# RG-LRU gates with high and low parts stacked in 128 rows, in a two-layer hybrid attention / RG-LRU / MLP step

## The chip, the cores and the metric

One core of one Trainium2 chip runs the whole step as one program. The metric is device time in microseconds (us); the kernel before takes 2474.3 us, the median of three runs (2474.01 to 2475.89).

## The reference

The step takes 1024 prompt frames, 32 frames of a running stream and 16 meta tokens through two layers. Each layer is: RMSNorm, one input projection, two parallel head groups, an output projection with a residual, then RMSNorm and a squared-ReLU MLP with a residual. One head group is latent attention. The other, the RG-LRU, is where the change lies:

```python
xc = p["conv_b"] + sum(xpad[:, k:k + T] * p["conv_w"][k] for k in range(CONV_W))
xb = xc.reshape(B, T, LRU_BLOCKS, LRU_BW)          # 8 blocks of 64 channels
r = sigmoid(einsum("btnc,ncd->btnd", xb, p["w_gate_a"]).reshape(B, T, LRU_W) + p["b_gate_a"])
i = sigmoid(einsum("btnc,ncd->btnd", xb, p["w_gate_x"]).reshape(B, T, LRU_W) + p["b_gate_x"])
log_a = -LRU_C * r * softplus(-p["lru_lambda"])
a = exp(log_a)
b = sqrt(-expm1(2.0 * log_a)) * (i * xc)
h_t = a_t * h_{t-1} + b_t                           # then y = h * gelu(g_r)
```

The two gates r and i are block-diagonal products: 8 blocks of 64 channels, each with its own 64 x 64 matrix for r and another for i.

## The kernel before

**Layout and precision.** All tokens of both request groups lie side by side as T = 1074 columns (1072 tokens and 2 columns of padding); channels lie on the 128 partitions. A product in fp32 is made of three fp32r passes (`PASSES`, L921): high weights by high data, high by low, low by high. "High" is the operand copied to fp32r, "low" what that copy left over. Each pass goes over the 1072 columns in three matmuls of 358, 358 and 356.

**Weight blocks.** Weights come in numbered blocks through two buffers, block b in buffer b % 2. SyncE loads a block to `raw_all` once the low half of the block before last is done, ScalarE copies its high half (`split`, L1496, semaphore `w_hi`) once TensorE is through with block b - 2, and VectorE subtracts for its low half (`split`, L2193, `w_lo`). `product` (L947) waits for the low half of its block, then for its place in PSUM, and makes all its passes.

**Units and slots.** The products of the mixer are numbered units. Units alternate between two PSUM slots of three banks each; `take(u)` (L931) makes unit u wait until unit u - 2 was read from the slot (the table `READ`). Banks 6 and 7 hold sums of squares.

**Order in the stretch of the gates** (the same in each layer; every engine has its own order written out by hand): TensorE runs the x_r products (XR), two gate-branch products (GR0, GR1), `gates(0)`, GR2, GR3, `gates(1)`, two latent products (CKV0, CKV1), `gates(2)`, the rotary-key product (`kr_product`, L1040: 48 matmuls on one block), CQ0, `gates(3)`, CQ1, CQ2, then a sum of squares for the latent (`sum_of_parts`, L988) and CQ3 to CQ5. A full product has 72 matmuls. c in `gates(c)` counts tiles of 128 channels, so each holds two blocks of 64: an even and an odd one.

**gates(c), L1006:** two products with a 128 x 128 weight each, one for r and one for i, with the two 64 x 64 matrices on the diagonal and zeros elsewhere: 2 x 3 x 3 = 18 matmuls, each gate in a slot of its own.

**ScalarE** (L1511 to L1618): `gate_r(c)` reads r from PSUM (Tanh, L1524), then makes Tanh (L1526) and Exp (L1528); `gate_i(c)` reads i (L1533) and makes a Sqrt (L1534, after a load of the activation table); `xc_hi(c+1)` makes the high part of the next tile of `xc`; `gelu_a`, `gelu_b` belong to the GeLU branch; `kr_lo` (L1606) reads half of the rotary keys; `split(b)` stand in between. **VectorE** (L2250 to L2391): `xc_lo(c)` (L2221) makes the low part of `xc`; `lru(c)` (L2258 to L2268) makes b and runs the scan; `scaled` evicts a product from PSUM (L2216); the eviction of the rotary keys (L2372, `kr_ev`) frees the slot that `gates(3)` takes next. **GpSimd** makes the GeLU's polynomial (`cube`, L3166 and L3168) for each tile.

**Between the layers** VectorE (L3105 to L3118) finishes the sums of squares of the new x with `next_sum(4..7)` (L3103) and then `next_split(1)` (L3096), the low half of layer 1's second weight block, for which TensorE's second product there waits.

Of the kernel before, what the change touches and what calls it, by code (L numbers as in the profile page):

```python
# [191 lines left out]

U_XR, U_GR, U_GATE, U_CKV = [0, 1, 2, 3], [4, 5, 8, 9], [6, 10, 14, 18], [12, 13]
U_KR, U_CQ = 16, [17, 20, 21, 22, 23, 24]
U_UQ, U_K, U_V = [25, 26, 27, 28, 29, 30], 31, 35
U_OY, U_OO, U_MLP = [45 + _c for _c in range(8)], 53, 61
NU = U_MLP
# [24 lines left out]
for _c in range(4):  # L222
    READ[U_XR[_c]] = ("xr_ev", _c + 1)
    READ[U_GR[_c]] = ("gr_ev", _c + 1)
    READ[U_GATE[_c]] = ("gate_r", _c + 1)
    READ[U_GATE[_c] + 1] = ("gate_i", _c + 1)
    READ[U_UQ[2 + _c]] = ("qn", _c + 1)
    READ[U_K + _c] = ("kf", _c + 1)
# [13 lines left out]
for _c in range(4):  # L242
    LAST_UNIT[B_XR[_c]] = U_XR[_c]
    LAST_UNIT[B_GR[_c]] = U_GR[_c]
    LAST_UNIT[B_GATE[_c]] = U_GATE[_c] + 1
    LAST_UNIT[B_OO + _c] = U_OO + 2 * _c + 1
# [171 lines left out]
def trunk(nc, xT, wst, vec, fgain, ropeC, ropeS, ident_in, past_ckv, past_kpe, h0, conv0,  # L418
          yT, ckv_out, kpe_out, h_out, conv_out, x_scr, sum_scr):
    ctx = ExitStack()  # L420
    with ctx:
# [17 lines left out]
        def tiles(name, region, first, n, dt=F32):  # L439
            return [place(f"{name}{i}", region, (first + i) * TB, T, dt) for i in range(n)]  # L440
# [479 lines left out]
        def _(pe):  # L920
# [5 lines left out]
            for L in range(DEPTH):  # L926
# [20 lines left out]
                def product(dst, u, b, woff, rhs_h, rhs_l, ready=None):  # L947

                    w("w_lo", b + 2)
                    take(u)  # L950
                    n = len(rhs_h)
                    for k in range(n):
                        if ready:
                            ready(k)
                        for i, (a, c) in enumerate(PASSES):
                            wt = (whi if a == "h" else wlo)[b % 2][:, woff + 128 * k:woff + 128 * k + 128]
                            r = (rhs_h if c == "h" else rhs_l)[k]
                            for q in range(3):
                                mm = nc.tensor.matmul(dst(q), wt, r(q), start=(k == 0 and i == 0), stop=(k == n - 1 and i == 2))  # L959
                    mm.then_inc(S["mm"], 1)  # L960
# [44 lines left out]

                def gates(c):  # L1006
                    w("xc_lo", c + 1)
                    for k in range(2):
                        product(to_slot(U_GATE[c] + k), U_GATE[c] + k, B_GATE[c], 128 * k, [tok(xch)], [tok(xcl)])

# [446 lines left out]
        def _(act):  # L1457
# [28 lines left out]
            for L in range(DEPTH):  # L1486
# [24 lines left out]
                def xc_hi(c):  # L1511
                    w("conv", c + 1)
                    if c:
                        w("mm", U_GATE[c - 1] + 2)
                    nc.scalar.activation(xch[:, :], xc[c][:, :], ACT.Copy).then_inc(S["xc_hi"], 1)

                def gate_r(c):

                    w("mm", U_GATE[c] + 1)
                    if c:  # L1520
                        w("hid", c)
                    else:
                        w("conv", 4)
                    nc.scalar.activation(chunks(t1), slot(U_GATE[c]), ACT.Tanh, scale=0.5, bias=half_ba[:, c:c + 1]).then_inc(S["gate_r"], 1)  # L1524
                    w("gate_r", c + 1)
                    nc.scalar.activation(t3[:, :], t1[:, :], ACT.Tanh, scale=sp2[:, c:c + 1], bias=sp2[:, c:c + 1]).then_inc(S["gate_y"], 1)  # L1526
                    w("gate_y", c + 1)
                    nc.scalar.activation(t1[:, :], t1[:, :], ACT.Exp, scale=neg_sp4[:, c:c + 1], bias=neg_sp4[:, c:c + 1]).then_inc(S["gate_t"], 1)  # L1528

                def gate_i(c):  # L1530

                    w("mm", U_GATE[c] + 2)
                    nc.scalar.activation(chunks(t4), slot(U_GATE[c] + 1), ACT.Tanh, scale=0.5, bias=half_bx[:, c:c + 1]).then_inc(S["gate_i"], 1)  # L1533
                    nc.scalar.activation(t3[:, :], t3[:, :], ACT.Sqrt).then_inc(S["root_t"], 1)  # L1534
# [49 lines left out]
                gate_r(0)  # L1584
                split(8)
                gate_i(0)
                xc_hi(1)
                split(9)
                gelu_a(0)
                gelu_b(0)  # L1590
                split(10)
                gate_r(1)
                split(11)
                gate_i(1)
                xc_hi(2)
                split(12)
                gelu_a(1)
# [5 lines left out]
                xc_hi(3)  # L1603
                split(15)
                w("mm", U_KR + 1)
                nc.scalar.activation(chunks(kpe[0:64, :]), slot(U_KR)[64:128], ACT.Copy).then_inc(S["kr_lo"], 1)  # L1606
                gelu_a(2)
                gelu_b(2)
                split(16)
                gate_r(3)  # L1610
                split(17)
                gate_i(3)
                for c in range(2):
# [527 lines left out]
        def _(dve):  # L2141
# [34 lines left out]
            for L in range(DEPTH):  # L2176
# [73 lines left out]
                def xc_lo(c):  # L2250
                    w("xc_hi", c + 1)
                    lo(xcl[:, :], xc[c][:, :], xch[:, :], "xc_lo")

# [94 lines left out]
                scaled(U_GR[1], g[1], rs, "gr_ev", LIVE)  # L2348
                split(7)
                split(8)  # L2350
                xc_lo(1)
                lru(0)
                split(9)
                scaled(U_GR[2], g[2], rs, "gr_ev", LIVE)
                scaled(U_GR[3], g[3], rs, "gr_ev", LIVE)
                split(10)
                gelu(0)
                split(11)
                xc_lo(2)
                lru(1)  # L2360
                split(12)
                scaled(U_CKV[0], ckv[0][:, 0:T], rs, "ckv_ev")
                scaled(U_CKV[1], ckv[1][:, 0:T], rs, "ckv_ev")
# [3 lines left out]
                xc_lo(3)  # L2367
                lru(2)
                split(15)
                w("mm", U_KR + 1)  # L2370
                w("kr_lo", 1)
                V.tensor_tensor(chunks(kpe[0:64, :]), slot(U_KR)[0:64], chunks(kpe[0:64, :]), ALU.add).then_inc(S["kr_ev"], 1)  # L2372
                scaled(U_CQ[0], cq[0], rs, "cq_ev", LIVE)
                split(16)
                gelu(2)
# [678 lines left out]
                def closing():  # L3054
# [30 lines left out]
                    if L < DEPTH - 1:  # L3085
# [386 lines left out]
```

## Time and profile before

| | |
|---|---|
| runs | 2474.01, 2474.3, 2475.89 us |
| the profiled execution | 2474.88 us, its span 2473.1 us |
| mean granted TensorE clock | 0.998 |

The span goes from the first to the last instruction; the execution's own time is 1.8 us more. In rows of the timeline the columns are start (us), length (us), engine, line, operation, output <- input, shapes, count, and in brackets the idle time before it with what ended it. Matmuls overlap: a matmul of 358 columns is listed with some 0.33 us, but the next starts much earlier, so their cost is read from one start to the next.

### The profile page before, as it was taken

To read this page: it belongs to the slowest core of one execution; us is meant where nothing else is said; L and a number is where in the kernel's file an instruction comes from. 1 tells how busy PE (TensorE), PEld (TensorE's weight loads), DVE (VectorE), ACT (ScalarE), POOL (GpSimd) and SP (SyncE) were. 2 spreads that over 40 slices of the span, in tenths; PEclk is the share of its full clock that TensorE was granted. 3 is DMA by queue.
4 is the path that set the end of the run, shared out by engine and by line. 5 is a ranking of instruction groups with operands and counts; after the bars stand their busy time and mean duration, and the time that the engine had idled before them with its cause. 6 is when DMAs were issued, how large, how long until landed. Compare 5 with 4: busy or idle time off the path is not lost.

```text
span 2473.1 us, 43928 instructions
## 1 busy us (share of the span) xinstructions
PE 2455.4 (99%) x17424; PEld 2371.3 (96%) x17424; DVE 1800.1 (73%) x2778; ACT 1219.7 (49%) x2197; POOL 515.9 (21%) x478
## 2 busy tenths in 40 slices
PE   9999999999999999999999999999999999999998
PEld 9999977899999999999999999779999999999997
DVE  8678767579776777677676797674887766776676
ACT  5455355535554454455524643555355544554455
POOL 0024255200112211220201232541001112211222
PEclk9999999999999999999999999999999999999999
DMA  4122201212447634663721222012135456545655
GB/s 160 55 60 73 61 11 38 86 59 107 89 91 140 122 86 99 135 119 89 226 89 52 63 70 61 11 38 90 60 115 103 91 120 131 110 89 115 131 113 173
DMA packets 104537, 230.39 MB, mean 93 GB/s; under 512 B 14816, under 2 KB 17984, under 8 KB 104336
## 3 DMA queue, kind: packets, MB, share of 16 engines
q0 software_dynamic: 43648, 89.14, 20.4%
q1 hardware_dynamic: 60544, 138.42, 17.6%
q8 instruction: 139, 2.28, 0.4%
q14 instruction: 62, 0.51, 0.1%
q10 hardware_dynamic: 144, 0.04, 0.0%
HBM read 144.03 MB, written 81.18 MB: 91 GB/s over the span
## 4 chain that ended last, share of the span: by engine, by line
PE 95%; DVE 3%; issue 1%; ACT 0%; DMA 0%; DVEq 0%; POOL 0%; ACTq 0%; POOLq 0%
PE ps L959 27%; PE ps L1303 23%; PE ps L1352 23%; PE ps L1167 5%; PE ps L1182 4%; PE ps L1444 3%; PE ps L1237 2%; PE ps L1415 2%; PE ps L1114 2%; PE ps L1026 1%; PE ps L1139 1%; DVE mxp L2518 0%; PE ps L1441 0%; PE ps L988 0%; DVE xall L2777 0%
## 5 line engine op out<-in xcount | busy, mean ns | idle before, releaser
L2808 DVE TENSOR_TENSOR wlo<-raw_all,whi 128x512 fp32r<-128x512 f32 (+1 forms) x420 | 270.9, 653 | 178.2 <-ACT whi L1973 175.7
L1973 ACT ACTIVATE whi<-raw_all 128x512 fp32r<-128x512 f32 (+1 forms) x420 | 248.6, 600 | 278.8 <-DVE raw_all L2941 87.8
L3307 POOL DMA_DIRECT2D x_scratch<-stage x224 | 199.6, 942 | 838.7 <-DVE stage L2951 694.3
L2026 ACT ACTIVATE stage<-ps 128x536 f32<-128x536 f32 (+1 forms) x224 | 135.4, 612 | 148.5 <-PE ps L1352 142.8
L1496 ACT ACTIVATE whi<-raw_all 128x1024 fp32r<-128x1024 f32 (+3 forms) x72 | 66.7, 926 | 233.9 <-PE ps L959 231.6
L2951 DVE TENSOR_TENSOR stage<-stage,ps 128x536 f32<-128x536 f32 (+1 forms) x168 | 119.0, 708 | 85.5 <-PE ps L1352 84.5
L2518 DVE TENSOR_REDUCE mxp<-ps 64x1 f32<-64x64 f32 (+11 forms) x384 | 140.4, 372 | 54.7 <-PE ps L1114 48.2
L959 PE MATMUL ps<-xgh,whi 128*128 128x358 f32 (+1 forms) x720 | 157.5, 327 | 1.8 <-DVE wlo L3096 1.7
L959 PE MATMUL ps<-xgl,whi 128*128 128x358 f32 (+1 forms) x720 | 156.6, 326 | 0.0
L959 PE MATMUL ps<-xgh,wlo 128*128 128x358 f32 (+1 forms) x720 | 156.5, 325 | 0.0
L959 PEld LDWEIGHTS ps<-xgh,whi 128*128 128x128 f32 x720 | 123.3, 189 | 2.6 <-DVE wlo L3096 2.0
L959 PEld LDWEIGHTS ps<-xgl,whi 128*128 128x128 f32 x720 | 124.1, 189 | 0.0
L959 PEld LDWEIGHTS ps<-xgh,wlo 128*128 128x128 f32 x720 | 123.3, 189 | 0.0
L2193 DVE TENSOR_TENSOR wlo<-raw_all,whi 128x1024 fp32r<-128x1024 f32 (+3 forms) x70 | 87.3, 1247 | 41.0 <-ACT whi L1496 40.6
L1167 PE MATMUL ps<-pn,v 128*65 128x320 f32 (+1 forms) x288 | 106.3, 453 | 0.0
L1754 ACT ACTIVATE pn<-ps 128x320 f32<-128x320 f32 (+1 forms) x144 | 65.4, 454 | 71.4 <-PE ps L1182 70.0
L1182 PE MATMUL ps<-qo,koh 128*128 128x320 f32 (+7 forms) x304 | 97.0, 400 | 0.0
L1182 PE MATMUL ps<-qe,keh 97*128 97x320 f32 (+7 forms) x304 | 95.7, 396 | 0.7 <-DMA qe<-mt 0.7
L2941 DVE TENSOR_TENSOR raw_all<-raw_all 128x256 f32<-128x256 f32 x224 | 89.7, 420 | 4.0 <-DMA raw_all<-in_wst 2.9
L1754 ACT ACTIVATE pd<-ps 16x64 f32<-16x64 f32 (+4 forms) x352 | 56.8, 224 | 55.4 <-PE ps L1182 55.1
L3292 POOL DMA_DIRECT2D raw_all<-in_wst x30 | 29.8, 992 | 254.2 <-DMA raw_all<-in_wst 254.2
L1182 PEld LDWEIGHTS ps<-qe,keh 97*128 97x128 f32 x304 | 54.7, 190 | 26.2 <-issue 7.2
(835 smaller groups left out, 7684.3 us busy)
## 6 DMA issues: line engine op xcount, KB each, us to landing
raw_all<-in_wst SPq DMA_DIRECT2D x232, 256.0 KB, 3.4
raw_all<-in_wst SPq DMA_DIRECT2D x80, 512.0 KB, 3.6
x_scratch<-stage POOLq DMA_DIRECT2D x112, 268.0 KB, 6.2
x_scratch<-stage POOLq DMA_DIRECT2D x112, 264.0 KB, 6.0
x_scratch<-xall POOLq DMA_DIRECT2D x24, 537.0 KB, 3.4
xall<-x_scratch SPq DMA_DIRECT2D x24, 537.0 KB, 9.4
xall<-in_xT SPq DMA_DIRECT2D x16, 537.0 KB, 7.2
raw_all<-in_wst POOLq DMA_DIRECT2D x30, 256.0 KB, 5.1
```

What stands on the lines that cost most here:

```text
L959: mm = nc.tensor.matmul(dst(q), wt, r(q), start=(k == 0 and i == 0), stop=(k == n - 1 and i == 2))
L1167: mm = nc.tensor.matmul(ps[0:65, bank, c0:c0 + n], v[:, v0:v0 + 65], p_tile(gk)[:, 0:n], start=(k in FIRST), stop=(k in LAST))
L1182: mm = nc.tensor.matmul(ps[:, gi % 3, 0:n], ks[e][0 if a == "h" else 1][rows, k0:k0 + P], qs[e][0 if c == "h" else 1][rows, q0:q0 + n], st ...
L1303: mm = nc.tensor.matmul(ps[:, 2 * slot_ + t, 0:HN], wt, rhs[:, t * HN:(t + 1) * HN], start=(opens and n == 0), stop=(n == 11), skip_group_ ...
L1352: mm = nc.tensor.matmul(ps[:, 2 * slot_ + t, 0:HN], ring(u, whi if a == "h" else wlo)[:, wc], fop[q, f + c][:, t * HN:(t + 1) * HN], start ...
L1754: ins = nc.scalar.activation(dst[r0:r1, c0:c1], src[r0:r1, c0:c1], ACT.Exp, scale=SM_SCALE)
L1973: nc.scalar.activation(dst, src, ACT.Copy).then_inc(S["u_hi"], 1)
L2026: nc.scalar.activation(quarters(stage_of(L, g, i, n)[:, 0:N2]), src, ACT.Copy, scale=-1.0 if row else 1.0).then_inc(S["x_copy"], 1)
L2518: ins = V.reduce_max(mxp[lo_:hi_, tile, part:part + 1], ps[lo_:hi_, max_bank(h, s), c0:c0 + n], AX_X)
L2808: V.tensor_tensor(dst, src, hi.bitcast(F32), ALU.subtract).then_inc(S["u_lo"], 1)
L2951: V.tensor_tensor(st, st, src, op).then_inc(S["x_add"], 1)
L3307: pool.dma_start(x_scr[2 * i + row, :, a:b], stage_of(L, g, i, n)[:, 0:b - a], accum_op=ALU.add).then_inc(S[done], 16)
```

## The change

The high and the low part of 64 channels of `xc` are stacked in 128 rows (`x_even` and `x_odd`, on the buffers of `xch` and `xcl`), against weights that hold the same 64 x 64 matrix twice, one above the other; the even block's weight has r and i side by side in its 128 columns, the odd block's has i and r. One pass with the high weights and one with the low ones then give both gates of 64 channels: 12 matmuls for `gates(c)` in place of 18. The odd block's results stand in the unit's slot; the even block's stand in banks 6 and 7 (512 columns each) and, for the last 48, in the rest of the slot's third bank. `gates(c)` is one unit, not two, so units are renumbered. Because r and i of a tile now lie half in one place and half in another, each gate is read by three ScalarE instructions (`gate`), `xc_hi` and `xc_lo` take two instructions each, and ScalarE reads both gates before it goes on with Tanh and Exp (`decay`) and Sqrt (`normal`). The orders of ScalarE and VectorE in the stretch are moved about. `product` waits for the high half of its block first and for the low half only before its third pass. Between the layers `next_split(1)` goes ahead of `next_sum(7)`. The diff, without the renumbering and the packing of weights and biases on the host:

```diff
@@ -626,6 +626,12 @@
 def half(e):
     return slice(64 * e, 64 * e + 64)
+
+
+def even_gates(c, end):
+
+    rest = ps[:, 3 * slot_of(U_GATE[c]) + 2, CH:CH + end - SUM_END]
+    return (ps[:, 6, :], 0, 512), (rest, SUM_END, end), (ps[:, 7, :], 512, SUM_END)
@@ -946,13 +952,15 @@
         def product(dst, u, b, woff, rhs_h, rhs_l, ready=None):
-            w("w_lo", b + 2)
+            w("w_hi", b + 1)
             take(u)
             n = len(rhs_h)
...
                     ready(k)
                 for i, (a, c) in enumerate(PASSES):
+                    if k == 0 and a == "l":
+                        w("w_lo", b + 2)
                     wt = (whi if a == "h" else wlo)[b % 2][:, woff + 128 * k:woff + 128 * k + 128]
                     r = (rhs_h if c == "h" else rhs_l)[k]
@@ -1004,9 +1012,21 @@
         def gates(c):
+            u, b = U_GATE[c], B_GATE[c]
             w("xc_lo", c + 1)
-            for k in range(2):
-                product(to_slot(U_GATE[c] + k), U_GATE[c] + k, B_GATE[c], 128 * k, [tok(xch)], [tok(xcl)])
+            w("w_lo", b + 2)
+            take(u)
+            if c:
+                w("gate_i", c)
+            else:
+                w("root", SUM_MIX)
+            for i, part in enumerate((whi, wlo)):
+                for dst, c0, c1 in even_gates(c, TOK):
+                    nc.tensor.matmul(dst, part[b % 2][:, 0:P], x_even[:, c0:c1], start=(i == 0), stop=(i == 1))
+            for i, part in enumerate((whi, wlo)):
+                for q in range(3):
+                    mm = nc.tensor.matmul(to_slot(u)(q), part[b % 2][:, P:2 * P], tok(x_odd)(q), start=(i == 0), stop=(i == 1))
+            mm.then_inc(S["mm"], 1)
         if L == 0:
@@ -1511,8 +1531,18 @@
             w("conv", c + 1)
             if c:
-                w("mm", U_GATE[c - 1] + 2)
-            nc.scalar.activation(xch[:, :], xc[c][:, :], ACT.Copy).then_inc(S["xc_hi"], 1)
+                w("mm", U_GATE[c - 1] + 1)
+            for e, dst in ((0, x_even), (1, x_odd)):
+                ins = nc.scalar.activation(dst[half(e), :], xc[c][half(e), :], ACT.Copy)
+            ins.then_inc(S["xc_hi"], 1)
+
+        def gate(c, dst, e, bias):
+
+            rest = even_gates(c, T)[1][0]
+            nc.scalar.activation(dst[0:64, 0:SUM_END].rearrange("p (c n) -> p c n", c=2), ps[half(e), 6:8, :], ACT.Tanh, scale=0.5,
+                                 bias=bias[half(e), c:c + 1])
+            nc.scalar.activation(dst[0:64, SUM_END:T], rest[half(e)], ACT.Tanh, scale=0.5, bias=bias[half(e), c:c + 1])
+            return nc.scalar.activation(chunks(dst[64:128, :]), slot(U_GATE[c])[half(1 - e)], ACT.Tanh, scale=0.5, bias=bias[half(1 - e), c:c + 1])
         def gate_r(c):
@@ -1521,16 +1551,21 @@
             else:
                 w("conv", 4)
-            nc.scalar.activation(chunks(t1), slot(U_GATE[c]), ACT.Tanh, scale=0.5, bias=half_ba[:, c:c + 1]).then_inc(S["gate_r"], 1)
+            gate(c, t1, 0, half_ba).then_inc(S["gate_r"], 1)
+
+        def gate_i(c):
+
+            gate(c, t4, 1, half_bx).then_inc(S["gate_i"], 1)
+
+        def decay(c):
+
             w("gate_r", c + 1)
             nc.scalar.activation(t3[:, :], t1[:, :], ACT.Tanh, scale=sp2[:, c:c + 1], bias=sp2[:, c:c + 1]).then_inc(S["gate_y"], 1)
...
             nc.scalar.activation(t1[:, :], t1[:, :], ACT.Exp, scale=neg_sp4[:, c:c + 1], bias=neg_sp4[:, c:c + 1]).then_inc(S["gate_t"], 1)
-        def gate_i(c):
-
-            w("mm", U_GATE[c] + 2)
-            nc.scalar.activation(chunks(t4), slot(U_GATE[c] + 1), ACT.Tanh, scale=0.5, bias=half_bx[:, c:c + 1]).then_inc(S["gate_i"], 1)
+        def normal(c):
+
             nc.scalar.activation(t3[:, :], t3[:, :], ACT.Sqrt).then_inc(S["root_t"], 1)
@@ -1582,17 +1617,21 @@
         split(7)
         gate_r(0)
-        split(8)
         gate_i(0)
         xc_hi(1)
+        split(8)
+        decay(0)
+        normal(0)
         split(9)
         gelu_a(0)
...
         split(10)
         gate_r(1)
-        split(11)
         gate_i(1)
         xc_hi(2)
+        split(11)
+        decay(1)
+        normal(1)
         split(12)
         gelu_a(1)
@@ -1601,15 +1640,19 @@
         gate_i(2)
         xc_hi(3)
-        split(15)
         w("mm", U_KR + 1)
         nc.scalar.activation(chunks(kpe[0:64, :]), slot(U_KR)[64:128], ACT.Copy).then_inc(S["kr_lo"], 1)
+        decay(2)
+        normal(2)
+        split(15)
         gelu_a(2)
         gelu_b(2)
         split(16)
         gate_r(3)
+        gate_i(3)
         split(17)
-        gate_i(3)
+        decay(3)
+        normal(3)
         for c in range(2):
             w("ckv_ev", c + 1)
@@ -2144,6 +2187,7 @@
     for s in (0, 1):
         V.memset(ps[:, 3 * s + 2, CH - 2:CH], 0.0)
+        V.memset(ps[:, 3 * s + 2, CH + TOK - 1024:CH + T - 1024], 0.0)
     V.memset(mx[:, :], 0.0).then_inc(S["const_set"], 1)
     lam = vecs[:, V_LAM:V_LAM + 4]
@@ -2249,7 +2293,8 @@
         def xc_lo(c):
             w("xc_hi", c + 1)
-            lo(xcl[:, :], xc[c][:, :], xch[:, :], "xc_lo")
+            V.tensor_tensor(x_even[half(1), :], xc[c][half(0), :], x_even[half(0), :].bitcast(F32), ALU.subtract)
+            V.tensor_tensor(x_odd[half(0), :], xc[c][half(1), :], x_odd[half(1), :].bitcast(F32), ALU.subtract).then_inc(S["xc_lo"], 1)
         def lru(c):
@@ -2347,31 +2392,31 @@
         scaled(U_GR[1], g[1], rs, "gr_ev", LIVE)
         split(7)
+        xc_lo(1)
         split(8)
-        xc_lo(1)
+        scaled(U_GR[2], g[2], rs, "gr_ev", LIVE)
         lru(0)
         split(9)
-        scaled(U_GR[2], g[2], rs, "gr_ev", LIVE)
         scaled(U_GR[3], g[3], rs, "gr_ev", LIVE)
         split(10)
         gelu(0)
+        xc_lo(2)
         split(11)
-        xc_lo(2)
+        scaled(U_CKV[0], ckv[0][:, 0:T], rs, "ckv_ev")
         lru(1)
         split(12)
-        scaled(U_CKV[0], ckv[0][:, 0:T], rs, "ckv_ev")
         scaled(U_CKV[1], ckv[1][:, 0:T], rs, "ckv_ev")
         split_kr()
...
         split(14)
         xc_lo(3)
-        lru(2)
-        split(15)
         w("mm", U_KR + 1)
         w("kr_lo", 1)
         V.tensor_tensor(chunks(kpe[0:64, :]), slot(U_KR)[0:64], chunks(kpe[0:64, :]), ALU.add).then_inc(S["kr_ev"], 1)
+        lru(2)
+        split(15)
+        split(16)
         scaled(U_CQ[0], cq[0], rs, "cq_ev", LIVE)
-        split(16)
         gelu(2)
         split(17)
@@ -3113,9 +3158,10 @@
                 next_sum(3)
                 next_low(7)
-                for m in (4, 5, 6, 7):
+                for m in (4, 5, 6):
                     next_sum(m)
                 next_split(1)
+                next_sum(7)
             else:
                 for n in range(6, 24):
```

## Rows read from the trace of the kernel before

**Rows 1.** The page's part 1: busy time, share of the span, instructions.
```profile
PE 2455.4 (99%) x17424; PEld 2371.3 (96%) x17424; DVE 1800.1 (73%) x2778; ACT 1219.7 (49%) x2197; POOL 515.9 (21%) x478
```

**Rows 2.** Timeline, TensorE, layer 0: gates(0) starts, GR2 starts.
```profile
80.30 1.14 PE L959 MATMUL ps<-xcs,whi 128*128 128x358 f32 x6
...
83.48 0.65 PE L959 MATMUL ps<-xgh,whi 128*128 128x358 f32 x3
```

**Rows 3.** Timeline, TensorE: starts of gates(2), kr, CQ0, gates(3), CQ1, sum.
```profile
133.86 1.14 PE L959 MATMUL ps<-xcs,whi 128*128 128x358 f32 x6
...
137.03 0.65 PE L1046 MATMUL ps<-xgh,whi 128*128 128x358 f32 x3
...
144.92 0.65 PE L959 MATMUL ps<-xgh,whi 128*128 128x358 f32 x3
...
156.97 1.23 PE L959 MATMUL ps<-xcs,whi 128*128 128x358 f32 x6
...
160.04 0.73 PE L959 MATMUL ps<-xgh,whi 128*128 128x358 f32 x3
...
183.73 1.23 PE L988 MATMUL ps<-xcs,ones_r 128*128 128x512 f32 x6
```

**Rows 4.** Timeline, TensorE, layer 1: gates(3) starts.
```profile
1388.03 1.22 PE L959 MATMUL ps<-xcs,whi 128*128 128x358 f32 x6 [0.15 <-DVE kpe L2372]
```

**Rows 5.** Timeline, TensorE, layer 0: fp32r matmuls of 512 and 50 columns, then XR2.
```profile
32.42 0.40 PE L988 MATMUL ps<-msq_r,ones_r 128*128 128x512 f32 x1
32.66 0.19 PE L988 MATMUL ps<-rs_r,ones_r 128*128 128x50 f32 x1
...
32.97 0.76 PE L959 MATMUL ps<-xgh,whi 128*128 128x358 f32 x3
```

**Rows 6.** Timeline, all engines, between the layers.
```profile
1244.13 5.42 DVE L3103 TENSOR_TENSOR msq<-msq,next_sq 128x1074 f32<-128x1074 f32 x4
...
1248.35 0.65 PE L959 MATMUL ps<-xgh,wlo 128*128 128x358 f32 x3
1249.47 1.22 DVE L3096 TENSOR_TENSOR wlo<-raw_all,whi 128x1024 fp32r<-128x1024 f32 x1
...
1250.74 0.76 PE L959 MATMUL ps<-xgh,whi 128*128 128x358 f32 x3 [1.75 <-DVE wlo L3096]
```

**Rows 7.** Groups by line and shape, ScalarE, 80 to 190 us: busy us, mean ns.
```profile
L1496 ACT ACTIVATE whi<-raw_all 128x1024 fp32r<-128x1024 f32 x10 | 10.5, 1052 | 26.4 <-PE ps L959 26.4
L1526 ACT ACTIVATE t<-t,sp 128x1074 f32<-128x1074 f32 x4 | 5.2, 1289 | 0.1
...
L1534 ACT ACT_TABLE_LOAD x4 | 5.1, 1283 | 0.1
...
L1524 ACT ACTIVATE t<-ps,half_ba 128x1074 f32<-128x1074 f32 x4 | 4.6, 1161 | 1.8 <-PE ps L959 1.8
...
L1534 ACT ACTIVATE t<-t 128x1074 f32<-128x1074 f32 x4 | 4.4, 1104 | 0.0
...
L1606 ACT ACTIVATE kpe<-ps 64x1074 f32<-64x1074 f32 x1 | 1.1, 1070 | 0.0
L1559 ACT ACTIVATE sqa<-ps,eps 128x50 f32<-128x50 f32 x1 | 0.3, 292 | 0.0
```

**Rows 8.** Timeline, VectorE, layer 0: lru(2), split(15), lru(3), the sum's low part.
```profile
145.96 1.27 DVE L2258 SCALAR_TENSOR_TENSOR t<-t,t 128x1074 f32<-128x1074 f32 x1
...
155.22 0.43 DVE L2193 TENSOR_TENSOR wlo<-raw_all,whi 128x256 fp32r<-128x256 f32 x1
...
167.05 1.28 DVE L2258 SCALAR_TENSOR_TENSOR t<-t,t 128x1074 f32<-128x1074 f32 x1 [2.31 <-ACT t L1534]
...
180.00 1.27 DVE L2221 TENSOR_TENSOR xcs<-sqa,xcs 128x1074 fp32r<-128x1074 f32 x1
```

**Rows 9.** Timeline, GpSimd, layer 0: the polynomial of tile 2.
```profile
149.59 2.99 POOL L3168 TENSOR_TENSOR t<-t,g 128x1074 f32<-128x1074 f32 x1
```

**Rows 10.** A stretch: us, PE, PEld, DVE, ACT, POOL busy, clock, DMA, GB/s.
```profile
1248.00:1251.00 3.00, 1.25 (x8) 0.96 (x7) 2.58 (x3) 0.00 (x0) 0.00 (x0) 1.00 0.00 0
```

More of the change, by code:

```diff
@@ L189 @@
 DONE_AT = [CLOSE_DOWN.index((_m, 0)) + 1 for _m in range(8)]
[L193 to L196, printed above, removed]
+U_XR, U_GR, U_GATE, U_CKV = [0, 1, 2, 3], [4, 5, 7, 8], [6, 9, 12, 15], [10, 11]
+U_KR, U_CQ = 13, [14, 16, 17, 18, 19, 20]
+U_UQ, U_K, U_V = [21, 22, 23, 24, 25, 26], 27, 31
+U_OY, U_OO, U_MLP = [41 + _c for _c in range(8)], 49, 57
 NU = U_MLP
@@ L224 @@
     READ[U_GR[_c]] = ("gr_ev", _c + 1)
-    READ[U_GATE[_c]] = ("gate_r", _c + 1)
-    READ[U_GATE[_c] + 1] = ("gate_i", _c + 1)
+    READ[U_GATE[_c]] = ("gate_i", _c + 1)
     READ[U_UQ[2 + _c]] = ("qn", _c + 1)
@@ L244 @@
     LAST_UNIT[B_GR[_c]] = U_GR[_c]
-    LAST_UNIT[B_GATE[_c]] = U_GATE[_c] + 1
+    LAST_UNIT[B_GATE[_c]] = U_GATE[_c]
     LAST_UNIT[B_OO + _c] = U_OO + 2 * _c + 1
@@ L460, in trunk @@
         xch, xcl = tiles("xcs", "X", 6, 2, F32R)
+        x_even, x_odd = xch, xcl
         sqa, sqt = tiles("sqa", "X", 6, 2)
@@ L3386 @@
             put(B_GR[c], block(w_in[:, s3 + P * c:s3 + P * c + P]))
-            gate = np.zeros((P, 2 * P), f32)
-            for n, name in enumerate(("w_gate_a", "w_gate_x")):
-                for i in range(2):
-                    gate[64 * i:64 * i + 64, P * n + 64 * i:P * n + 64 * i + 64] = a[name][l, 2 * c + i]
-            put(B_GATE[c], gate)
+            even = [a[name][l, 2 * c] for name in ("w_gate_a", "w_gate_x")]
+            odd = [a[name][l, 2 * c + 1] for name in ("w_gate_x", "w_gate_a")]
+            put(B_GATE[c], np.tile(np.concatenate(even + odd, 1), (2, 1)))
         for c in range(2):
@@ L3436 @@
         parts = [cols(a["norm_mix_g"][l]), cols(a["q_norm_g"][l]), cols(a["kv_norm_g"][l]), cw, cols(a["conv_b"][l]), cols(a["b_gate_a"][l]),
-                 cols(a["b_gate_x"][l]), cols(a["lru_lambda"][l]), cols(a["attn_out_g"][l]), cols(a["lru_out_g"][l]), cols(a["norm_mlp_g"][l]),
+                 np.roll(cols(a["b_gate_x"][l]), P // 2, 0), cols(a["lru_lambda"][l]), cols(a["attn_out_g"][l]), cols(a["lru_out_g"][l]), cols(a["norm_mlp_g"][l]),
                  cols(a["norm_mix_g"][min(l + 1, DEPTH - 1)])]
```

## The prediction

> **What bounds the kernel now.** I read the page's busy times first: TensorE is busy for 2455.4 of 2473.1 us, VectorE for 1800.1, ScalarE for 1219.7 [rows 1]. So TensorE is the path nearly everywhere, a matmul taken away is time won, and a wait of TensorE is time lost. The view of who waited for whom then names few waits of TensorE in the stretches that change. One is between the layers, before layer 1's second product, for the low half of its weights [rows 6]; another is before gates(3), for the eviction of the rotary keys [rows 3, 4]. Last I laid the timelines of the engines beside each other in the stretch of the gates, because the change moves more on ScalarE and VectorE there than on TensorE.
>
> **What is taken from TensorE.** From its start to the next product gates(0) takes 83.48 - 80.30 = 3.18 us [rows 2], gates(2) 3.17 and gates(3) 3.07 [rows 3]; with gates(1) taken as gates(2), 12.59 us a layer. Afterwards it has six matmuls of the old width at 0.164 us (kr's 48 take 7.89 us [rows 3]), 0.98 us, and four of 512 columns at 0.24 us (32.42 to 32.66 [rows 5]), 0.96 us. Two of 48 columns are left. The nearest rows have two of 50 columns one behind the other, 0.31 us together, with the next product's start in it [rows 5]. Below, such a matmul costs almost nothing beyond its columns; above, 0.155 us each. I take 0.05, nearer the lower end, because here each one stands behind a 512-column matmul and not behind another short one. That is 2.05 us for a gate, 2.25 at the upper end. Saved: 12.59 - 4 x 2.05 = 4.4 us a layer, 8.8 in both. (The Trainium skill, "TensorE: Matmul & The Clock Gate", section on LDWEIGHTS, puts a load of 128 weight columns at about 107 ns, which 48 columns don't cover; by that, an estimate, a gate would be 0.1 us dearer and the kernel 0.9. The rows' sum doesn't use it.)
>
> The wait before gates(3) goes as well: CQ0 opens at 144.92, gates(3) at 156.97, 12.05 us later, while CQ1 and CQ2 take (183.73 - 160.04)/2 = 11.85 each [rows 3]; layer 1 shows the same wait [rows 4]. That is 0.25 us a layer, 0.5 in both.
>
> **Between the layers.** TensorE's last pass there opens at 1248.35 and should take 0.49; the next product opens at 1250.74, so 1.90 us are lost, until `next_split(1)` (1249.47 + 1.22) is done [rows 6]. Moved ahead of one sum (5.42 us for four, 1.35 each [rows 6]), the split is done by 1249.35, and its low half is now due only after two passes, at 1249.8. All 1.90 us go. The sum that moves back ends by 1250.7; TensorE asks for it after two of the eight tiles, at about 1251.8, so it stays hidden.
>
> Gains: 8.8 + 0.5 + 1.9 = 11.2 us.
>
> **What is put in the way.** Count from the start of gates(2), layer 0. TensorE: gates to 2.05; kr (7.89) and 0.1 for the half subtraction of kr's weights, which is due earlier now, to 10.05; CQ0 (11.8) to 21.85. There it wants gates(3), whose low weights are block 15. (For the 0.1: below nothing, above the 0.25 of the wait just named.)
>
> ScalarE: a gate's read is three instructions instead of one. Two have some 1.16 us, as the read of 1074 columns has now, and the short one 0.29; half the partitions are no discount (64 partitions x 1074: 1.07) [rows 7]. That is 2.6 us a gate against 1.16. From 2.05 on it makes r (2.6), split(14) (1.05), i (2.6), and the next tile's high part, now in two instructions of 1.07: 10.45. Only then comes `kr_lo` (1.07), kr being ready at 10.05, and only then Tanh 1.29, Exp 1.29, table load 1.28 and Sqrt 1.10 [rows 7]: 16.5, less some handing over and overlap that about cancel; I take 16.4. Before, the reads and these four were done when lru(2) began, at 145.96 - 133.86 = 12.1 [rows 8].
>
> VectorE: lru(2) needs that Sqrt, and split(15) stands right behind lru(2) in its order. From lru(2) to the end of split(15) it is 155.22 + 0.43 - 145.96 = 9.7 us [rows 8]. So block 15's low half is there at 26.1, and TensorE, which was at gates(3) by 21.85, **waits 4.25 us**. Before, the same point was reached at 21.8 against 22.9: the order is the same, but what feeds it is later and what asks for it is earlier. In the 9.7 us is a collision with GpSimd, whose second instruction takes 2.99 us in the middle of it [rows 9]; without it 6.7 would be left and a wait of 1.25. The polynomial still starts just behind split(15) of ScalarE, so it falls into lru(2) again; I take 9.7. Two layers: 8.5 us, at least 2.5.
>
> Behind it: CQ1 needs CQ0 evicted, and split(16) now stands ahead of that eviction; 1.22 [rows 6] and 1.28 (the nearest row of that size [rows 8]) against 2.05 of gates: 0.45 us. And the sum of squares after CQ2: its low part was done at 181.27 [rows 8], TensorE came at 183.73 [rows 3], 2.46 spare. Both gates' reads (2 x 2.6 for 2 x 1.16) delay lru(3) by some 3.0 us against the start of gates(3), and TensorE comes 0.65 earlier (1.0 less for the gates, 0.45 back at CQ1, 0.1 less at CQ1's start): 1.2 us of wait; bounds 0 and 2.4, as GpSimd's collisions fall.
>
> Waits put in: 0.1 + 4.25 + 0.45 + 1.2 = 6.0 us a layer, **12.0 in both**.
>
> At no cost: `gates(1)` and `gates(2)` have the same chain, but GR2 (CKV0) is evicted at 15.2 and 9.7 us more give 24.9, against 2 x 11.8 + 2.05 = 25.65 on TensorE; cover 0.75, and what exceeds it is paid. The waits for the high half come sooner than the old ones; all products but the one between the layers found theirs met. The doubled `xc_lo` lies under the 11.8 us of a product. Two small memsets at the start: under 0.2 us.
>
> **The sum.** 2474.9 (the profiled execution) - 11.2 + 12.0 = 2475.7. That execution is 0.6 above the median of the runs, so I forecast 2475.0, no change that can be told: this kernel's measurement tells about 0.2%, 4.9 us, from no change. The case's own range, with a wait at gates(3) of 2.5 to 5 us and the bounds above: 2470 to 2479.
>
> **Rivals.** *The reads stay hidden (faster).* If lru(2) and split(15) are done about when TensorE asks, because GpSimd doesn't collide or ScalarE's reads are shorter, the gains stand alone: 2474.3 - 11.2 = 2463.1, or 2466 with the lower bound of the wait. For it: ScalarE is busy for half the span [rows 1]. Against it: the chain is in one order on two strict queues, and it would have to be 4 us shorter.
>
> *The clock falls (slower).* TensorE has no idle of 4 us in these stretches now. With 1.25 us of work in 3.00 the granted clock stayed at 1.00, which is 2.4 GHz [rows 10]; nothing shows what it does after 4.25 us of idle before each gates(3). (The same page of the Trainium skill, section "Why this matters for your kernels", asks for no idle gaps of that kind between bursts, or the clock goes back to half; no trace here shows it.) At 1.2 GHz each pass of 0.49 us would take about twice that. If it lasted for 6 us, half of CQ1, each layer would lose 3 us more: 2481. It decides only where the gap is as long as worked out, and the granted clock just behind it is under 1.00.
>
> *The stack doesn't save a third.* If the short matmuls and the longer ones show their weight loads, 2.25 us a gate: 1.6 us more, 2476.6, within the first case's range.
>
> **How the numbers follow.** First case, with the third rival in it: 0.68; hidden reads 0.22; clock 0.10. The first case reaches past 0.2% on each side a little. Faster 0.23, same 0.63, slower 0.14. The range takes in most of the faster rival and of the clock's: 2464 to 2480.
>
> **What would show it.** Right: gates at 2.0 to 2.25 us; the second product of layer 1 opening without a wait; TensorE idle 3.5 to 5 us before gates(3) in both layers, released by VectorE's low half at L2193's place; smaller waits before CQ1 and the sum. Wrong: no wait at gates(3) (then the first rival), or a wait before gates(1), where I see 0.75 us of cover, or a granted clock below 1.00 after it.

## The result and the profile after

The changed kernel takes 2487.43 us (median of six runs, 2486.36 to 2488.76) against 2474.89 for six runs of the kernel before: ratio 1.005, interval 1.0041 to 1.006. It is **slower**, by 12.5 us (0.5%), and lies above the predicted range. The profiled execution took 2488.0 us, its span 2486.2, so 13.1 more than before. TensorE is busy about as long, although 48 matmuls are gone; ScalarE and VectorE have some 31 and 19 us more to do (to be held against [rows 1]):

```profile
PE 2454.4 (99%) x17376; PEld 2367.4 (95%) x17376; DVE 1818.8 (73%) x2788; ACT 1251.1 (50%) x2237; POOL 514.7 (21%) x478
```

TensorE's timeline in layer 0: gates(0) to GR2, gates(2), kr, CQ0 with its last pass, gates(3), CQ1, CQ2, the sum, and UQ0 to the sum behind it. (UQ0 is the first product that takes the results of CQ0 to CQ5 as its input.)

```profile
80.47 0.73 PE L1025 MATMUL ps<-xcs,whi 128*128 128x512 f32 x3
...
82.61 0.66 PE L967 MATMUL ps<-xgh,whi 128*128 128x358 f32 x3
...
132.23 0.82 PE L1025 MATMUL ps<-xcs,whi 128*128 128x512 f32 x3
...
134.45 0.66 PE L1066 MATMUL ps<-xgh,whi 128*128 128x358 f32 x3
...
142.31 0.65 PE L967 MATMUL ps<-xgh,whi 128*128 128x358 f32 x3
...
153.62 0.65 PE L967 MATMUL ps<-xgh,wlo 128*128 128x358 f32 x3
159.12 1.40 PE L1025 MATMUL ps<-xcs,whi 128*128 128x512 f32 x3 [4.84 <-issue]
...
163.17 1.09 PE L967 MATMUL ps<-xgh,whi 128*128 128x358 f32 x3
...
188.32 1.35 PE L996 MATMUL ps<-xcs,ones_r 128*128 128x512 f32 x6 [0.29 <-DVE xcs L2265]
...
225.01 0.66 PE L967 MATMUL ps<-cqh,whi 128*128 128x358 f32 x3
...
229.28 0.75 PE L967 MATMUL ps<-cqh,whi 128*128 128x358 f32 x3 [1.13 <-DVE cql L2267]
...
234.86 0.76 PE L967 MATMUL ps<-cqh,whi 128*128 128x358 f32 x3 [0.89 <-DVE cql L2267]
...
236.44 1.22 PE L996 MATMUL ps<-t_r,ones_r 128*128 128x512 f32 x6
```

Read it from start to start against [rows 2, 3]. gates(0) takes 82.61 - 80.47 = 2.14 us in place of 3.18, as planned. CQ0 to gates(3) takes 16.81 in place of 12.05: its last pass should end at 153.62 + 0.49, so TensorE stands for 5.0 us. And gates(3), with the same 12 matmuls as gates(0), takes 163.17 - 159.12 = 4.05. The stretches show why. Each line has its bounds and length in us, then the busy time of PE, PEld, DVE, ACT and POOL, then the granted clock (1.00 is full speed).

```profile
148.00:153.95 5.95, 5.95 (x39) 5.95 (x37) 4.71 (x3) 3.66 (x4) 3.41 (x2) 1.00 0.00 0
153.95:159.12 5.17, 0.33 (x3) 0.06 (x2) 5.07 (x7) 2.04 (x2) 0.68 (x1) 0.96 0.00 0
159.12:165.50 6.38, 6.38 (x20) 5.99 (x21) 4.68 (x4) 2.08 (x3) 0.00 (x0) 0.50 0.52 164
165.50:170.00 4.50, 4.50 (x29) 4.50 (x28) 0.52 (x1) 4.44 (x6) 0.00 (x0) 1.00 0.01 4
...
1394.90:1401.00 6.10, 6.10 (x19) 5.71 (x20) 4.62 (x4) 1.79 (x3) 0.00 (x0) 0.50 0.55 175
```

Behind the idle the granted clock is 0.50, 1.2 GHz, for 6.4 us in layer 0 and 6.1 in layer 1, and half of that is lost: some 3.1 us a layer. Nothing in VectorE's timeline is a surprise; lru(2) starts late and is in front of split(15) (the 256-column one of the two instructions that the last line puts together):

```profile
149.17 1.28 DVE L2303 SCALAR_TENSOR_TENSOR t<-t,t 128x1074 f32<-128x1074 f32 x1 [2.36 <-ACT t L1569]
150.49 2.20 DVE L2305 SCALAR_TENSOR_TENSOR t<-t,xc 128x1074 f32<-128x1074 f32 x1
152.72 3.05 DVE L2306 SCALAR_TENSOR_TENSOR t<-t,t 128x1074 f32<-128x1074 f32 x1
155.80 2.33 DVE L2308 TENSOR_TENSOR_SCAN xc<-t,t 128x1040 f32<-128x1040 f32 x1
...
158.59 1.56 DVE L2237 TENSOR_TENSOR wlo<-raw_all,whi 128x256 fp32r<-128x256 f32 x2
```

The view of what TensorE waited for (us in total, times, longest) has both layers. "issue" in the first line is the idle at gates(3), whose end the profile put to no engine; lining up the timelines gives split(15), and the runs below confirm it.

```profile
PE ps L1025 <- issue: 9.7, 2, 4.9
PE ps L967 <- DVE cql L2267: 4.0, 4, 1.1
...
PE ps L996 <- DVE xcs L2265: 0.8, 2, 0.5
```

The second line is new too: UQ0 stands for the low parts of its own input. It takes 236.44 - 225.01 = 11.43 us; in the kernel before it had no wait and took 8.90:

```profile
220.29 0.66 PE L959 MATMUL ps<-cqh,whi 128*128 128x358 f32 x3
...
229.19 1.23 PE L988 MATMUL ps<-t_r,ones_r 128*128 128x512 f32 x6
```

Between the layers the wait is gone. Layer 1's second product opens at 1255.79, one pass behind 1255.30, and its low pass, at 1256.77, finds the split done (1255.05 + 1.22):

```profile
1255.30 0.65 PE L967 MATMUL ps<-xgh,wlo 128*128 128x358 f32 x3
1255.79 0.65 PE L967 MATMUL ps<-xgh,whi 128*128 128x358 f32 x3
...
1256.77 0.65 PE L967 MATMUL ps<-xgh,wlo 128*128 128x358 f32 x3
```
```profile
1255.05 1.22 DVE L3141 TENSOR_TENSOR wlo<-raw_all,whi 128x1024 fp32r<-128x1024 f32 x1
```

Added up for layer 0 from the start of gates(0) to the end of UQ0: gates(0) to gates(2) gain about 1 us each; CQ0 with the idle behind it loses 4.76, gates(3) 0.98 (it should have gained 0.93), CQ1 and CQ2 lose 1.5, UQ0 2.5. Layer 1 has the same within 0.2 us. That is 7 us lost a layer, 2 gained between them, and some 1 us spread over the rest.

### The profile page after: what moved, and what is told of

Same layout as the page of the kernel before. It is cut to its first block, busy times and chain, and to the rows that moved or that the text cites. A ratio compares the mean times of both kernels' runs of the same rounds, so it can differ in the third digit from the quotient of the medians.

```text
span 2486.2 us, 43882 instructions
## 1 busy us (share of the span) xinstructions
PE 2454.4 (99%) x17376; PEld 2367.4 (95%) x17376; DVE 1818.8 (73%) x2788; ACT 1251.1 (50%) x2237; POOL 514.7 (21%) x478
## 4 chain that ended last, share of the span: by engine, by line
PE 90%; DVE 6%; ACT 2%; issue 1%; DMA 1%; POOL 0%; SPq 0%; DVEq 0%; POOLq 0%; ACTq 0%
PE ps L1372 23%; PE ps L1323 23%; PE ps L967 22%; PE ps L1187 5%; PE ps L1202 4%; PE ps L1464 3%; PE ps L1257 2%; PE ps L1134 2%; PE ps L1435 1%; PE ps L1046 1%; PE ps L1159 1%; DVE cql L2267 1%; PE ps L1066 1%; PE ps L1025 0%; DVE xall L2822 0%
## 5 line engine op out<-in xcount | busy, mean ns | idle before, releaser
L2237 DVE TENSOR_TENSOR wlo<-raw_all,whi 128x1024 fp32r<-128x1024 f32 (+3 forms) x70 | 79.4, 1137 | 40.0 <-ACT whi L1516 39.3
L1202 PEld LDWEIGHTS ps<-qo,koh 128*128 128x128 f32 x304 | 54.8, 189 | 25.9 <-issue 5.2
```

The lines of the kernel that those rows point to most:

```text
L1202: mm = nc.tensor.matmul(ps[:, gi % 3, 0:n], ks[e][0 if a == "h" else 1][rows, k0:k0 + P], qs[e][0 if c == "h" else 1][rows, q0:q0 + n], st ...
```

## The experiments

The theory after the traces: **A**, gates(3) is late because VectorE and ScalarE reach the end of tile 2 late; each such idle of TensorE costs twice, as idle and as a lowered clock behind it; and the lateness travels down VectorE's order to the sum and to UQ0. The rivals: **B**, only block 15's place in the order is wrong; or the clock fell for another reason than the idle. Each ratio below is against runs of the kernel before that were made together with that run (their medians lie between 2474.36 and 2475.52).

| run | us, median | ratio to before, interval |
|---|---|---|
| changed kernel | 2487.43 | 1.005 (1.0041 to 1.006) |
| fill | 2483.87 | 1.0035 (1.0021 to 1.005) |
| split15 | 2479.62 | 1.0017 (1.0007 to 1.0026) |
| cube_later | 2482.93 | 1.0031 (1.0019 to 1.0044) |
| boundary | 2473.26, one run | read from the trace |
| open_lru | 2481.05 | 1.0022 (1.0013 to 1.0032) |
| early_sum | 2481.47 | 1.0025 (1.0016 to 1.0035) |
| early_rstd | 2473.14 | 0.9993 (0.9983 to 1.0003) |
| early_kpe | 2466.11 | 0.9963 (0.9949 to 0.9977) |

**fill: the wait kept, the idle filled.**

```diff
 def gates(c):
     w("xc_lo", c + 1)
-    w("w_lo", b + 2)
     take(u)
...
+    for _ in range(18 if c == 3 else 0):
+        nc.tensor.matmul(ps[:, 6, :], ones_r[:, :], xgh[0][:, 0:512], start=True, stop=True)
+    w("w_lo", b + 2)
```

> The changed kernel with 18 extra matmuls of 512 columns on TensorE just ahead of the wait for block 15's low half, before gates(3); they write zeros-free scratch sums into bank 6, which gates(3) overwrites. Work is added, none removed; the wait's end (VectorE's split(15) at about 159.0 us) is untouched. Theory A (the idle before gates(3) costs twice, once as idle and once as a lowered clock behind it): the extra matmuls take 18 x 0.22 = 3.9 us of the 5.0, the idle that is left is about 1 us, the granted clock behind it stays at 1.00, gates(3) takes 2.1 us in place of 4.05 and CQ1 11.8 in place of 12.9, so 3 us a layer come back: about 2481.5 us. Theory B (the clock falls for another reason, for example the shape of the gates' matmuls): clock 0.50 behind it as before, 2487 to 2488 us.

gates(3) still waits for split(15), now named as the releaser, but the clock stays at 1.00 and gates(3) takes 2.4 us. TensorE's timeline, then a stretch:

```profile
154.29 4.37 PE L1023 MATMUL ps<-xgh,ones_r 128*128 128x512 f32 x18
159.25 0.85 PE L1027 MATMUL ps<-xcs,whi 128*128 128x512 f32 x3 [0.59 <-DVE wlo L2239]
...
161.67 0.73 PE L967 MATMUL ps<-xgh,whi 128*128 128x358 f32 x3
```
```profile
159.00:162.00 3.00, 2.73 (x14) 2.29 (x15) 3.00 (x4) 0.31 (x1) 0.00 (x0) 1.00 0.54 152
```

The span falls from 2486.2 to 2481.3 with work *added*. So the idle lowered the clock, not the gates' form. The median is 2.4 us above what A expected: TensorE now comes earlier to the sum and waits there for 2.3 us in all in place of 0.8, which is 1.5 of it. The waits at UQ0 stay as they were, 4.0 us in all.

**split15: block 15 ahead of lru(2).**

```diff
 ScalarE:                        VectorE:
+    split(15)                  +    split(15)
     decay(2)                        lru(2)
     normal(2)                  -    split(15)
-    split(15)                       split(16)
```

> The changed kernel with split(15) ahead of lru(2) on VectorE and ahead of decay(2) on ScalarE, nothing else moved. Theory A (VectorE's whole tile is late, block 15 is only the first thing that is asked of it): gates(3) opens without a wait at about 154 us, but CQ0's eviction still stands behind lru(2) and split(16), done at about 161.3, so CQ1 waits about 5 us, the clock falls behind that wait, and the time stays within 2 us of the changed kernel: 2485 to 2489. Theory B (block 15 alone was in the way): no idle over 1.5 us in the stretch, 8 us a layer come back: about 2471.

The wait moved, as A had it: gates(3) opens without one, and CQ1 stands for CQ0's eviction behind lru(2).

```profile
161.57 1.23 PE L967 MATMUL ps<-xgh,whi 128*128 128x358 f32 x3 [4.91 <-DVE cq L2260]
```
```profile
161.50:165.10 3.60, 3.53 (x13) 3.56 (x14) 2.60 (x3) 3.56 (x5) 0.00 (x0) 0.58 0.41 137
```

Yet the time is 5.4 us below A's lowest. The larger part of that is the waits at the sum and at UQ0, 0.8 and some 5 us in both layers, which are gone: gates(3) itself was on time, so lru(3) starts at 169.87 and not, as in the changed kernel, at 174.47. fill is the run to hold against it: there TensorE opens the sum at 186.60 as it does here, but gates(3) opens at 159.25 in place of 154.37, and UQ0 waits. UQ0's stall was therefore a late consequence of gates(3)' delay. Neither expectation had said so. The smaller part is the clock: it was at 0.50 for 3.0 us of the stretch above, and for 4.8 us in layer 1 behind a wait of the same length, against 6.4 and 6.1 in the changed kernel.

```profile
1391.93 1.22 PE L967 MATMUL ps<-xgh,whi 128*128 128x352 f32 x3 [4.92 <-DVE cq L2260]
```

**cube_later: GpSimd's polynomial out of lru(2).**

```diff
     split(15)
+    split(16)
     gelu_a(2)
     gelu_b(2)
-    split(16)
```

> The changed kernel with ScalarE's split(16) ahead of gelu_a(2) and gelu_b(2), so that GpSimd's polynomial of tile 2 starts about 6 us later, behind most of lru(2). If the collision with GpSimd makes some 2.7 us of lru(2), as the prediction had it: the second and third steps of lru(2) take 1.3 us each in place of 2.2 and 3.05, block 15's low half comes at about 156.4, TensorE idles 2.3 us before gates(3) in place of 5.0. If the clock still falls behind 2.3 us: 2 x 2.6 less, about 2482. If it stays at 1.00: 3 us a layer more, about 2476. If the collision is not what lengthens lru(2): idle of 5 us and 2487.

Without GpSimd beside it the third step of lru(2) takes 1.28 us, not 3.05, and TensorE idles for 2.15 us. Behind that the clock is 1.00. VectorE, TensorE and a stretch:

```profile
151.32 1.28 DVE L2306 SCALAR_TENSOR_TENSOR t<-t,t 128x1074 f32<-128x1074 f32 x1
```
```profile
155.94 0.82 PE L1025 MATMUL ps<-xcs,whi 128*128 128x512 f32 x3 [2.15 <-issue]
...
186.15 2.33 PE L996 MATMUL ps<-xcs,ones_r 128*128 128x512 f32 x6 [3.99 <-DVE xcs L2265]
```
```profile
156.00:162.00 6.00, 6.00 (x34) 5.56 (x35) 2.88 (x3) 3.06 (x3) 4.02 (x2) 1.00 0.54 175
...
186.10:192.00 5.90, 5.85 (x18) 5.47 (x19) 2.83 (x4) 3.35 (x4) 1.21 (x1) 0.50 0.28 87
```

So the collision is worth 2.7 us of the 4.84. But the time fell by 4.5 us only, not by 11: gelu_b(2) is late now, gate_r(3) stands behind it on ScalarE, and the sum waits 3.99 us, again with half the clock behind it. (In layer 1 it waits 4.07 us, and the clock is at 0.50 for 3.4 us in place of 5.9.)

**boundary: the kernel before, with one line moved,** as in the change, and the product's wait left as it was.

```diff
-    for m in (4, 5, 6, 7):
+    for m in (4, 5, 6):
         next_sum(m)
     next_split(1)
+    next_sum(7)
```

> The kernel before with next_split(1) ahead of next_sum(7) and nothing else (the product still waits for its low half before its first pass). The low half is then there at about 1249.35 us and the product is asked for at 1248.84, so of the 1.9 us lost between the layers about 0.5 stays: TensorE waits 0.4 to 0.6 there, and the span is about 1.4 us shorter than before, 2471.7 us, which one run's time can't tell but its trace can.

The split starts at 1249.02; the product opens 0.52 us behind the end of the last pass (1249.28 + 0.49), and the span is 2471.5, 1.6 less:

```profile
1250.29 0.76 PE L959 MATMUL ps<-xgh,whi 128*128 128x358 f32 x3 [0.36 <-DVE wlo L3096]
```

The move is worth three quarters of the 1.9 us, the later wait the rest.

**open_lru: CQ0's eviction and split(16) inside lru(2).** On the kernel of split15:

```diff
+    lru(2, lambda: (scaled(U_CQ[0], cq[0], rs, "cq_ev", LIVE), split(16)))
-    lru(2)
-    split(16)
-    scaled(U_CQ[0], cq[0], rs, "cq_ev", LIVE)
 ScalarE:
     gelu_a(2)
+    split(16)
     gelu_b(2)
-    split(16)
```

> The kernel of split15 with lru(2) opened up: CQ0's eviction and split(16) stand between its second and third step on VectorE, and split(16) ahead of gelu_b(2) on ScalarE. CQ0's eviction is then done at about 155.7 us and split(16) at 156.9; TensorE asks for them at 156.5 and 157.5. So TensorE should wait nowhere from gates(2) to the sum of squares, with a granted clock of 1.00 throughout: 6.4 us a layer come back (4.9 of idle, 1.5 of lowered clock). Theory A (VectorE and ScalarE are late by a whole chain, so the wait moves on): lru(3) starts at about 172, and the sum's low part behind it is done at about 184, while TensorE is there at 180.2: a wait of 3 to 4.5 us before the sum of squares, and 1 to 2.5 us for the low parts of UQ0; 2474 to 2478 us. Theory B (two places were in the way and no more): 2467 us.

No wait is left from gates(2) to CQ2. Everything collects before the sum (the waits of both layers, and the stretch behind one):

```profile
PE ps L996 <- DVE xcs L2265: 11.0, 2, 5.6
```
```profile
185.60:191.50 5.90, 5.87 (x18) 5.50 (x19) 2.83 (x4) 3.37 (x4) 1.22 (x1) 0.50 0.27 88
```

5.5 us of idle a layer, and 3 of clock: A's mechanism, with a larger wait than expected and the clock left out of my sum once more. B falls.

**early_sum: the sum's chain ahead of lru(3).** On the kernel of open_lru, ScalarE's order and VectorE's as they now stand (the moved steps are marked; "squares" are the latent's, behind a wait for gates(3)):

```diff
 ScalarE:                        VectorE:
     gelu_b(2)                       gelu(2)
+    squares                         split(17)
     gate_r(3)                  +    lo(xch, sqa, xcl, "sum_lo")
     gate_i(3)                  +    scaled(U_CQ[1], cq[1], rs, "cq_ev", LIVE)
     split(17)                  +    split(18)
+    sum's high part                 lru(3)
+    split(18)                       gelu(3)
     decay(3)
     normal(3)
     gelu_a(3)
```

> The kernel of open_lru with the chain of the latent's sum of squares moved ahead of lru(3): ScalarE's squares behind gelu_b(2), its high part and split(18) ahead of decay(3), and VectorE's low part, CQ1's eviction and split(18) ahead of lru(3). The low part is then there at about 169.6 us, so the wait before the sum of squares goes. Theory A: lru(3) and gelu(3) end about 5 us later against TensorE than in split15 (about 186 against a sum at 180.9), what follows them on ScalarE (squares of y, split(19), the latent's rstd) and on VectorE up to the low parts of UQ0 is late with them, and UQ0 waits 3 to 6 us in all: 2472 to 2478. Theory B: nothing waits at UQ0: 2467.

The wait at the sum is gone, and has become over 10 us of others: CQ4 and UQ0 wait for the evictions of CQ2 and CQ4, and UQ0 then for its low parts.

```profile
PE ps L967 <- DVE cq L2261: 6.0, 3, 2.5
PE ps L967 <- DVE cql L2268: 4.3, 4, 1.9
```
```profile
221.12 1.23 PE L967 MATMUL ps<-cqh,whi 128*128 128x358 f32 x3 [2.46 <-DVE cq L2261]
```

UQ0's waits, 4.0 and 5.2 us in the two layers, are what A had, but the time is 3.5 us above its range: CQ4's wait of 1.0 us a layer was not in it, nor was the clock. Behind the 2.46 us in layer 0 the clock is 0.50 for 2.9 us; behind 2.44 us in the same place of layer 1 it stays at 1.00.

**early_rstd: the latent's rstd ahead of the squares of y.** On the kernel of early_sum, ScalarE:

```diff
+    split(19)
+    log_rstd(SUM_KV, sqt, KVL)
     y_square(0)
     y_square(1)
-    split(19)
-    log_rstd(SUM_KV, sqt, KVL)
```

> The kernel of early_sum with ScalarE's split(19) and the latent's rstd ahead of the first two squares of y, so that VectorE's 3 to 4.5 us of idle behind gelu(3) are filled. Theory A: the wait at UQ0 falls by 3 to 4.5 us a layer against early_sum: 2466 to 2470. If the wait at UQ0 is set by VectorE's work alone and not by what it waits for on ScalarE: the same time as early_sum.

8.3 us less: the waits for the evictions are gone, so they hung on what VectorE stood waiting for on ScalarE. But the time is 3.1 us above A's range, since 5.2 us of waits for the low parts stay (1.77 + 0.89 in layer 0), and it cannot be told from that of the kernel before. Before them VectorE turns the rotary key, beside GpSimd's sums; its product with the cosine takes 3.04 us:

```profile
PE ps L967 <- DVE cql L2268: 5.2, 4, 1.8
```
```profile
205.32 3.04 DVE L2336 TENSOR_TENSOR kpe<-kpe,rope 64x1074 f32<-64x1074 f32 x1
```

**early_kpe: the rotary key's work into VectorE's idle.** On the kernel of early_rstd, VectorE (the same steps taken out behind split(20); the added waits for semaphores are left out here):

```diff
     split(15)
+    link(V.tensor_tensor(kpe[0:64, 0:T], kpe[0:64, 0:T], rs[0:64, :], ALU.mult))
     lru(2, ...)
     gelu(2)
     split(17)
+    rotate(kpe[0:64, 0:T], t2[0:64, :], cosT[0:64, :], sinT[0:64, :], None)
+    link(V.tensor_copy(kpe[64:96, 0:T], kpe[0:32, 0:T]))
     w("sum_hi", SUM_KV)
```

On ScalarE `split(17)` goes ahead of gate_r(3), and gelu_a(3) waits for the sum's low part (it shares t2).

> The kernel of early_rstd with split(17) ahead of gate_r(3) on ScalarE, and on VectorE the rotary key's scaling between split(15) and lru(2) and its rotation and copy (with t2 in place of t1 as their scratch) between split(17) and the sum's low part, where VectorE idled 3.3 and 2.2 us; later, where they stood, they took some 13 us because GpSimd's sums ran beside them. Theory A (the 2.9 us of waits at UQ0 are VectorE's own lateness): the waits for UQ0's low parts and for split(17) go, 3.2 + 0.7 us a layer, 7.7 in both: span 2463 to 2465 and 2465 to 2467 us, faster than the kernel before by 0.3 to 0.4%. If the low parts of UQ0 are late because of CQ5's eviction and ScalarE's high parts instead, 2471 to 2473.

2466.11 us, 0.37% under the kernel before, and as A expected it. TensorE waits nowhere from gates(2) to UQ0; gates(3) opens one pass behind CQ0 and UQ0 takes 225.32 - 216.43 = 8.89 us, as in the kernel before, where the changed kernel took 11.43. The cosine's product takes 1.27:

```profile
153.62 0.65 PE L967 MATMUL ps<-xgh,wlo 128*128 128x358 f32 x3
154.11 0.73 PE L1025 MATMUL ps<-xcs,whi 128*128 128x512 f32 x3
...
156.25 0.66 PE L967 MATMUL ps<-xgh,whi 128*128 128x358 f32 x3
...
216.43 0.66 PE L967 MATMUL ps<-cqh,whi 128*128 128x358 f32 x3
...
225.32 1.23 PE L996 MATMUL ps<-t_r,ones_r 128*128 128x512 f32 x6
```
```profile
168.94 1.27 DVE L2337 TENSOR_TENSOR kpe<-kpe,rope 64x1074 f32<-64x1074 f32 x1
```

The gains of the change were there all along: this kernel, with the same stacked gates, is 9.4 us faster than the one before, of the 11.2 that the prediction counted as gains. Could the new orders alone have done it, without the stacked gates? The kernel before leaves them next to nothing to win: in this stretch TensorE waits there for 0.25 us a layer, before gates(3). And from the start of gates(0) to the end of UQ0 layer 0 takes 225.32 - 80.48 = 144.84 us here against 229.19 - 80.30 = 148.89 there; the 4.05 us between them are about four gates at 1.0 each. Not tried: the stacked gates with the orders of the kernel before left as they were; the units' slots differ, and several evictions must move with them.

## Why the prediction was wrong

- **The gates: right.** 2.05 us forecast, 2.14 measured. The 0.05 us I took for a matmul of 48 columns was too little: 0.98 + 0.96 for the long ones leave 0.10 each. That is what the estimate from the Trainium skill had given ("TensorE: Matmul & The Clock Gate", section on LDWEIGHTS: 0.1 us dearer a gate); the rows I went by, with their upper end at 0.155, left it open.
- **Between the layers: right**, all 1.9 us, and boundary shows the move's share.
- **The wait at gates(3): right in place and cause, small in size.** 4.25 us forecast, 5.0 measured. TensorE came at 154.11 - 132.23 = 21.9 us behind the start of gates(2), as worked out (21.85); block 15 was ready some 0.7 us later than the 26.1, for the most part because lru(2) began at 16.9 and not at 16.4, and the rest is the handing over. cube_later put GpSimd's share at 2.7, where the prediction had 3.0.
- **The step that failed: the wait was priced as idle time only.** "TensorE waits 4.25 us" went into the sum with 4.25, and what it does to the clock stood as a rival with 0.10, although that rival's condition, a gap of that length, was what my main case forecast. A granted clock below 1.00 behind the wait was also named there as a sign of being wrong, and it came. The rival's price was right, with luck: its 6 us of low clock, 3 us a layer, were assumed and not worked out; measured 6.4 and 6.1 us at 0.50, while waits of 4.1 to 4.9 us in cube_later and split15 had only 3.0 to 4.8 us of it. The row that I set against it, clock 1.00 in a stretch with 1.75 us of idle [rows 6, 10], was a shorter gap and said nothing of 4 us. fill shows the cause: with the idle filled the clock stays at 1.00. (The Trainium skill's page "TensorE: Matmul & The Clock Gate", section "Why this matters for your kernels", asks for no such gaps; here trace and page agree.)
- **The second failure: VectorE's lateness was followed to the sum and no farther.** Forecast there 1.2 us, measured 0.3 and 0.5; in fill, where the clock stays up, 1.1 and 1.2, so the size was right and the fallen clock hid part of it. UQ0 stood in no step, and lost 2.5 us a layer. split15, where gates(3) is on time, has no wait at UQ0, and early_kpe shows that VectorE's own work in front of the low parts sets it.
- **CQ1's wait of 0.45: not there.** gates(3), at the lowered clock, took 4.05 us, and CQ0's eviction was done in that time. In fill, at the full clock, CQ1 opens 0.17 us late (161.67 against 161.01 + 0.49).
- **Before gates(2): a small wait, forecast at nothing.** The prediction saw 0.75 us of cover. CKV1's last pass opens at 131.49 and should take 0.49, gates(2) opens at 132.23, 0.25 us late, just behind block 12's low half (VectorE, 131.70 + 0.43); in layer 1 it is 0.17.
- **Together:** 2475.7 for the profiled execution was forecast. Add 3.1 a layer for the clock, 2.5 for UQ0, 0.7 at gates(3), and take off some 0.8 at the sum and 0.45 at CQ1, twice: 2485.8, against 2488.0. The 0.09 us of each gate, 0.7 for all eight, and the 0.4 before gates(2) are in the gap, and the rest of it is small steps that no row singles out.

## What to carry to other kernels

Price a forecast wait of the engine that bounds by what comes behind it as well: here 5 us of idle cost 8, and 18 useless matmuls in it gave 4.9 us of the span back. If that is the main case, it can't be a rival's 1 in 10. When an operation of the bounding engine gets cheaper and its helpers dearer, walk the helpers' order to the next place where they are idle, for every wait on the way; mending the first wait here only moved it, four times, and what helped in the end was bringing forward what a helper stood waiting for (early_rstd, 8.3 us) and moving work that nobody waits for yet into a helper's idle time (early_kpe, another 7).

## What the runs showed of the hardware

- The granted clock behind an idle of TensorE, layer 0 / layer 1. Behind 0.6 us (fill) and 2.15 / 2.24 us (cube_later, gates(3)) it was 1.00. Behind 2.46 / 2.44 us (early_sum, UQ0) it was 0.50 for 2.9 us / 1.00. Then 0.50 for: 5.9 / 3.4 us behind 3.99 / 4.07 us (cube_later, the sum); 6.4 / 6.1 behind 4.84 / 4.86 (the changed kernel); 3.0 / 4.8 behind 4.91 / 4.92 (split15); some 6 / 5.4 behind 5.44 / 5.58 (open_lru). So each of the listed idles from 3.99 us on was followed by the lower clock and cost 1.5 to 3.2 us beyond itself, and not more the longer it was; what sets the length stays open.
- VectorE beside GpSimd: the third step of lru(2) took 3.05 us beside GpSimd's product and 1.28 alone, the rotary key's product with the cosine 3.04 and 1.27. In both cases it ended 1.1 us behind GpSimd's instruction (155.77 against 154.63 in the changed kernel, 208.36 against 207.23 in early_rstd). (The Trainium skill, "GPSIMD Engine Reference", section "Key points", says that the two engines share their interfaces to SBUF; the runs agree with that, though they show only the longer times.)
